# The last 512 MLP features: from two sets of seven products to a plain down projection, half of it woven into the last set and half by token tiles with the final norm and the store

## The reference, cut to what matters

```python
    hf = rms_norm(x, norm_mlp[l])
    x = x + jnp.square(jax.nn.relu(hf @ w_up[l])) @ w_down[l]
return rms_norm(x, norm_final)
```

## Time and profile before

| what | value |
|---|---|
| median of 3 runs | 2890.66 us |
| the profiled execution's own time | 2890.3 us |
| its span (first to last instruction) | 2888.5 us |
| TensorE (PE) busy with matmuls | 98% of the span |
| DVE, ACT, POOL busy | 56%, 35%, 15% |
| mean granted TensorE clock | 0.995 |

### The profile page before, as it was taken

One profiled execution on the slowest core, in us unless ns is written; L12 is line 12 of the kernel. 1 busy time (PEld: TensorE's weight loads), 2 busy tenths in 40 slices (PEclk: granted clock), 3 DMA queues, 4 the chain that ended last, 5 costly groups with the idle time before them and its releaser, 6 DMA issues.

```text
span 2888.5 us, 33862 instructions
## 1 busy us (share of the span) xinstructions
PE 2833.9 (98%) x12753; PEld 2322.8 (80%) x12753; DVE 1626.3 (56%) x2089; ACT 1018.1 (35%) x1383; POOL 431.0 (15%) x262
## 2 busy tenths in 40 slices
PE   8999999999999999999999999999999999999995
PEld 7888877777788888888878888888888888888874
DVE  6212245444325656632344677777677777777677
ACT  6222234333232223322344333333433333343333
POOL 1000000000000000000000332233223331333233
PEclk9999999999999999999999999999999999999998
DMA  7332222322233232553212233223332333223312
GB/s 264 102 102 90 97 90 102 102 87 102 101 117 102 88 109 95 172 177 102 88 59 88 73 117 117 90 96 105 116 104 85 102 116 116 76 98 116 116 59 102
DMA packets 132034, 306.27 MB, mean 106 GB/s; under 512 B 7561, under 2 KB 7674, under 8 KB 129530
## 3 DMA queue, kind: packets, MB, share of 16 engines
q1 hardware_dynamic: 130522, 294.80, 30.6%
q10 hardware_dynamic: 1440, 10.49, 0.9%
HBM read 290.58 MB, written 14.68 MB: 106 GB/s over the span
## 4 chain that ended last, share of the span: by engine, by line
PE 95%; DVE 2%; ACT 1%; issue 1%; DMA 1%; POOL 1%; SPq 0%; POOLq 0%; DVEq 0%; ACTq 0%
PE acc L1603 16%; PE acc L1605 15%; PE acc L1604 15%; PE acc L1931 8%; PE acc L1929 8%; PE acc L1930 8%; PE aux L1949 6%; PE aux L1951 6%; PE aux L1953 6%; PE aux L1624 1%; PE aux L1699 1%; DVE xs L1471 1%; PE aux L1716 1%; PE aux L1698 1%; DMA wide<-in_w_down 0%
## 5 line engine op out<-in xcount | busy, mean ns | idle before, releaser
L981 DVE TENSOR_TENSOR wlo<-raw,whi 128x2048 fp32r<-128x2048 f32 x128 | 293.2, 2290 | 487.3 <-ACT whi L592 486.2
L1603 PE MATMUL acc<-act_hi,whi 128*128 128x512 f32 x1088 | 435.8, 401 | 0.5 <-DVE act_lo L985 0.5
L1605 PE MATMUL acc<-act_hi,wlo 128*128 128x512 f32 x1088 | 424.9, 391 | 0.0
L1604 PE MATMUL acc<-act_lo,whi 128*128 128x512 f32 x1088 | 424.1, 390 | 0.0
L1412 DVE TENSOR_TENSOR flo<-wide,fhi 128x1024 fp32r<-128x1024 f32 x192 | 263.7, 1374 | 250.1 <-ACT fhi L866 250.0
L1929 PE MATMUL acc<-act_hi,fhi 128*128 128x512 f32 x1024 | 398.7, 389 | 0.0
L1931 PE MATMUL acc<-act_hi,flo 128*128 128x512 f32 x1024 | 398.4, 389 | 0.0
L1930 PE MATMUL acc<-act_lo,fhi 128*128 128x512 f32 x1024 | 398.4, 389 | 0.0
L592 ACT ACTIVATE whi<-raw 128x2048 fp32r<-128x2048 f32 x128 | 244.5, 1910 | 436.2 <-PE acc L1605 427.1
L866 ACT ACTIVATE fhi<-wide 128x1024 fp32r<-128x1024 f32 x192 | 203.7, 1061 | 530.4 <-PE acc L1931 363.2
L1949 PE MATMUL aux<-fhi,P_hi 128*128 128x512 f32 x896 | 351.0, 392 | 14.7 <-DVE xs L1471 14.6
(11 more groups left out here) (286 smaller groups left out, 4090.3 us busy)
## 6 DMA issues: line engine op xcount, KB each, us to landing
raw<-in_w_in SPq DMA_DIRECT2D x80, 1024.0 KB, 5.0
raw<-in_w_up SPq DMA_DIRECT2D x64, 1024.0 KB, 5.3
wide<-in_w_down SPq DMA_DIRECT2D x64, 1024.0 KB, 5.2
raw<-in_w_out SPq DMA_DIRECT2D x16, 1024.0 KB, 5.4
gates_scratch<-gate_out ACTq DMA_DIRECT2D x10, 1024.0 KB, 3.9
raw<-in_w_ckv SPq DMA_DIRECT2D x8, 1024.0 KB, 12.1
xs<-in_x SPq DMA_DIRECT2D x8, 1024.0 KB, 13.2
raw<-in_w_attn_br SPq DMA_DIRECT2D x8, 1024.0 KB, 8.2
```

The source lines that it names most:

```text
L981: nc.vector.tensor_tensor(wlo[n % 2][:], raw[n % 4][:], whi[n % 2][:].bitcast(F32), ALU.subtract).then_inc(lo_ready, 1)
L1603: nc.tensor.matmul(dst, s_hi, v_hi, start=first, stop=False)
L1604: nc.tensor.matmul(dst, s_hi, v_lo, start=False, stop=False)
L1605: ins = nc.tensor.matmul(dst, s_lo, v_hi, start=False, stop=last)
```

## The change

Chunk 15 no longer uses the seven products. Its down projection is the plain one: 4 token tiles x 4 feature blocks x 4 column blocks x 3 matmuls.

- **Set 1** of round 7 gets the list `LAST`: its seven products with four units `Y` between and behind them. The `Y` units compute the left half of the outputs (columns 0 to 1023) for chunk 15: 24 matmuls each, into the four `acc` banks, which held the up projection. `Y0` and `Y1` make columns 0 to 511, `Y2` and `Y3` columns 512 to 1023; `land_plain` on DVE adds each of the two halves to `xs` in four pieces.
- **Sets 2 and 3 are gone.** In their place the right half (columns 1024 to 2047) is computed token tile by token tile (`m`): 24 matmuls for each of four tiles, into two banks of its own for each (`z_banks`), from four ring entries z = 0 to 3 that all tiles share. Behind each tile DVE lands it, ACT squares it, POOL makes its inverse root, and the tile is scaled and stored: the left half by ACT (`left_scale`, after DVE multiplied it by the gain), the right by DVE in one operation with the gain (`right_scale`).
- The token operand of the plain product is `hid` split as a whole, `plain_hi` (ACT) and `plain_lo` (DVE), four pieces each. The side sums and splits of chunk 15 and the weight sums of sets 2 and 3 are gone.
- ACT: in set 1 `hidden` stands behind the hi split of P7, at position 4, where it stood ahead of it. DVE: the landings of set 1 are placed by a table `LANDS`, two units behind the product instead of four.
- SP: the four loads of `w_down` for chunk 15 go to slots 0 and 1 during set 0 (in the place of `load_up`), then slot 2 behind P5's split, and slot 3 behind P3's; `gain_f` is loaded between these two. Stores go tile by tile, left then right.

The matmuls from the start of set 1 on are 84 + 96 + 96 = 276 in place of 21 x 12 = 252.

The order, and the banks of the right half:

```diff
+LAST = ("P1", "P2", "P6", "P7", "P5", "Y", "P4", "Y", "P3", "Y", "Y")
+C_LAST = 2 * FF_ROUNDS + 1
...
+    z_banks = (aux[0:2], aux[2:4], acc[0:2], acc[2:4])
```

On SP, in the sets, at the end of the round and behind it:

```diff
+            sp.wait_ge(unit_lo, before + 9)
+            if last and s == 1:
+                load_down(0, C_LAST, 0, 0)
...
+            sp.wait_ge(unit_lo, before + 11)
+            if last and s == 1:
+                load_down(1, C_LAST, 1, 0)
...
+        sp.wait_ge(unit_lo, first + LAST.index("P5") + 1)
+        load_down(2, C_LAST, 0, 1)
+        sp.wait_ge(unit_used, first)
         sp.dma_start(gain_f[:], norm_final.partition_broadcast(P)).then_inc(fin_loaded, 16)
...
+        sp.wait_ge(unit_lo, first + LAST.index("P3") + 1)
+        load_down(3, C_LAST, 1, 1)
+        for t in range(NT):
+            sp.wait_ge(out_left, t + 1)
+            sp.dma_start(out_v[:, t, 0:D // 2], xs[:, t, 0:D // 2]).then_inc(out_stored, 16)
+            sp.wait_ge(out_right, t + 1)
+            sp.dma_start(out_v[:, t, D // 2:D], xs[:, t, D // 2:D]).then_inc(out_stored, 16)
```

On ACT, in the sets and behind them:

```diff
-                if s % 2 and pos == 3 and not (last and s == 3):
+                if s % 2 and pos == (4 if last else 3):
                     hidden(c + 1, first - 1, t)
...
+                if last and s == 1 and name == "P5":
+                    for k in range(4):
+                        act.wait_ge(hid_ready, c * 4 + (4 + k + 1))
+                        nc.scalar.activation(plain_hi[:, k, :], hid[:, k, :], ACT.Copy).then_inc(side_hi, 1)
...
+        for m in range(NT):
+            act.wait_ge(y_landed, NT + m + 1)
+            nc.scalar.activation(junk_l[m][:], xs[:, m, 0:D // 2], ACT.Square, accum_out=x_sums[:, m, 0:1]).then_inc(x3_sq, 1)
...
+        for m in range(NT):
+            for j in range(2):
+                act.wait_ge(z_landed, 2 * m + j + 1)
+                nc.scalar.activation(junk_r[2 * m + j][:], xs[:, m, cols(2 + j, BLK)], ACT.Square,
+                                     accum_out=x_sums[:, m, 1 + j:2 + j]).then_inc(x3_sq, 1)
+            if m:
+                left_scale(m - 1)
+        left_scale(NT - 1)
```

On DVE, the table of landings, and what follows set 1:

```diff
+        LANDS = {"P2": ("P4",), "P6": ("P3",), "P5": ("P1", "P2"), "P4": ("P7",), "P3": (), "Y0": ("P6",), "Y1": ("P5",), "Y2": ("P4",)}
...
+        land_plain(0)
+        for z in range(4):
+            unit_split_lo(set_first(2) + z, wide[2 + z % 2][:, :, cols(z // 2, BLK)], FF_ROUNDS)
+            if z == 0:
+                land("P3", set_first(1) + LAST.index("P3"), 1, FF_ROUNDS)
+        land_plain(1)
...
+        for m in range(NT):
+            dve.wait_ge(z_full, m + 1)
+            for j in range(2):
+                nc.vector.scalar_tensor_tensor(out=xs[:, m, cols(2 + j, BLK)], in0=z_banks[m][j][:], scalar=m_inv[:, m:m + 1],
+                                               in1=xs[:, m, cols(2 + j, BLK)], op0=ALU.mult, op1=ALU.add).then_inc(z_landed, 1)
+            if m == 0:
+                left_gain(0)
+            if m < NT - 1:
+                left_gain(m + 1)
+            dve.wait_ge(x3_sq, NT + 2 * m + 2)
+            nc.vector.reduce_sum(f_sum[:, m:m + 1], x_sums[:, m, 0:3], AX).then_inc(f_stat, 1)
+            if m:
+                right_scale(m - 1)
+        right_scale(NT - 1)
```

On PE, the four token tiles of the right half (its three matmuls for each k are those of the `Y` units):

```diff
+        for m in range(NT):
+            if m < 2:
+                pe.wait_ge(pair_free, landed + 13 + m)
+            else:
+                pe.wait_ge(y_landed, NT + 2 * m - 2)
+            for z in range(4):
+                half, g = z // 2, z % 2
+                n = set_first(2) + z
+                if m == 0:
+                    pe.wait_ge(unit_lo, FF_ROUNDS * PER_ROUND + n + 1)
```

More of the change, by code:

```diff
@@ new lines, in _ @@
+        for s in range(4):
+            down_set(0, s)
+        with sp.Fori(1, FF_ROUNDS) as t:
+            for s in range(4):
+                down_set(t, s)
+        for s in range(2):
+            down_set(FF_ROUNDS, s, last=True)
+        first = FF_ROUNDS * PER_ROUND + set_first(1)
+        sp.wait_ge(unit_lo, first + LAST.index("P5") + 1)
+        load_down(2, C_LAST, 0, 1)
+        sp.wait_ge(unit_used, first)
+        sp.dma_start(gain_f[:], norm_final.partition_broadcast(P)).then_inc(fin_loaded, 16)
@@ L928, in down_set @@
         def down_set(t, s, last=False):
-            first, units, c = set_first(s, last), set_units(s, last), 2 * t + s // 2
+            first, units, c = set_first(s), set_units(s, last), 2 * t + s // 2
             up = 0
@@ L1515, in down_set @@
                         side_split_lo("P3", c)
-                if s % 2 and not last:
+                else:
                     if pos == 5:
@@ new lines, in _ @@
+        up = 0
+        for pos, name in enumerate(LAST):
+            n = set_first(1) + pos
+            for done in LANDS.get(f"Y{up}" if name == "Y" else name, ()):
+                if pos < 3:
+                    land(done, set_first(0) + WITH_UP.index(done), 0, FF_ROUNDS)
+                else:
+                    land(done, set_first(1) + LAST.index(done), 1, FF_ROUNDS)
+            if name == "Y":
+                if up == 0:
+                    for k in range(4):
+                        dve.wait_ge(side_hi, C_LAST * 7 + k + 1)
+                        nc.vector.tensor_tensor(plain_lo[:, k, :], hid[:, k, :], plain_hi[:, k, :].bitcast(F32), ALU.subtract).then_inc(side_lo, 1)
+                unit_split_lo(n, wide[up % 2][:, :, cols(up // 2, BLK)], FF_ROUNDS)
+                up += 1
+            else:
+                unit_split_lo(n, t2[:] if name == "P6" else quarter(1, name), FF_ROUNDS)
@@ L1971, in _ @@
             up_unit(8 + u, u, 1)
-        down_round(0)
+        for s in range(4):
+            down_set(0, s)
         with pe.Fori(1, FF_ROUNDS) as t:
-            down_round(t)
-        down_round(FF_ROUNDS, last=True)
+            for s in range(4):
+                down_set(t, s)
+        for s in range(2):
+            down_set(FF_ROUNDS, s, last=True)
+        landed = 2 + 28 * FF_ROUNDS
+        for m in range(NT):
+            if m < 2:
+                pe.wait_ge(pair_free, landed + 13 + m)
+            else:
+                pe.wait_ge(y_landed, NT + 2 * m - 2)
+            for z in range(4):
+                half, g = z // 2, z % 2
+                n = set_first(2) + z
+                if m == 0:
+                    pe.wait_ge(unit_lo, FF_ROUNDS * PER_ROUND + n + 1)
+                r, bank = n % RING, z_banks[m][half]
+                for i in range(2):
+                    k = 2 * g + i
+                    nc.tensor.matmul(bank[:], plain_hi[:, k, cols(m)], fhi[r][:, i, :], start=k == 0, stop=False)
+                    nc.tensor.matmul(bank[:], plain_hi[:, k, cols(m)], flo[r][:, i, :], start=False, stop=False)
+                    ins = nc.tensor.matmul(bank[:], plain_lo[:, k, cols(m)], fhi[r][:, i, :], start=False, stop=k == 3)
+            ins.then_inc(z_full, 1)
     ctx.close()
```

191 lines of the change are left out of this document (93 added, 98 removed).

## The result

The changed kernel takes **2864.91 us** (median, 2863.91 to 2865.63, 4 runs) against 2890.49 (2890.07 to 2893.11, 4 runs): a ratio of 0.9909, 95% interval 0.9892 to 0.9927. It is 25.6 us faster. The profiled execution has a span of 2863.9 us for the 2888.5 of before.

What follows compares the result with a forecast made beforehand. The prediction took PE as the bound except for 21.1 us lost between products and the tail. Terms +5.4 matmuls, -20.7 lost time and -10.1 tail gave -25.3 us, 2865.4 us, range 2862 to 2876.

Steps and rivals of the forecast that it cites:

- PE's work: Last chunk's matmuls on PE: 168 taken out, 96 + 96 put in, 24 more, +5.4 us.
- The wait at P6: Set 1 of round 7: PE still waits 0.35 us of 1.28, as P7's split on DVE ends behind POOL's T4.
- Y0, the tightest place: First plain unit in set 1: DVE's split ends at 2802.7, PE asks at 2803.0, 0.3 us to spare.
- PE through: Last matmul: PE ends at 2852.05, 15.2 us earlier than 2867.26.
- The tail: Last matmul to the end: 11.2 us for 21.2, since three of four tiles are normed and stored under matmuls.
- POOL's two steps: In the last tile's norm: taken at 2.78 us, with 1.91 as the shorter bound.
- the scaling: DVE's last scaling with the gain, in the tail: taken at 1.22 us, bounds 1.22 and 1.40.
- The sum: Whole kernel: -15.2 and -10.1 make -25.3 us, 2865.4 against the median.
- the 21.1 us: PE time lost between the 21 products of sets 1 to 3: 14.6 us of waits, the rest slower matmuls behind them.
- The first rival: Waits stay in the last set: 1.0 us for each of seven products, +7, 2872; chance 0.08.
- The second rival: The tail stays serial because a step taken as covered isn't: it keeps its 21.2 us, 2875.5; chance 0.06.
- The two slower ones: PE is full, so added work adds time: 2896, chance 0.02; plain matmuls step at 0.43 by the clock: 2904, chance 0.03.

Runs made afterwards that it cites:

- the doubled tile: Changed kernel with the 24 matmuls of token tile 1 done twice, result unchanged: 2869.97 us.
- products in a row: Changed kernel with the last set's seven products in a row, then the four plain units, landings moved to match: 2864.72 us.
- the 11.1 that the run gave: Changed kernel, but DVE waits for all four token tiles before landing the first, so norm and stores follow the last matmul: 2875.06 us.
- moving one line: Kernel before, with DVE's wait for ACT's eight squares moved behind the landing of P7 in the last set: 2884.95 us.
- the first step of the shorter tail: Changed kernel with PE signalling each of a tile's two banks and tile 2's scaling ahead of the last landing: 2863.43 us.
- without side work: Kernel before, without chunk 15's token-side sums and hi/lo splits on ACT and DVE: 2882.93 us.

## Why the prediction was right

**PE's work.** +5.4 us by 24 matmuls of 0.227; the doubled tile showed +5.4.

**The wait at P6.** 0.35 us predicted behind the pace, 0.35 measured (2796.31 for 2795.96), for the reason given: T4 on POOL and then P7's split. Undoing ACT's order gave +0.95 for the 0.9 of the working.

**Y0, the tightest place.** Its split was to end 13.75 us from set 1, wanted at 14.05: measured 13.8 and 14.05. PE did not wait.

**PE through.** 63.1 us from set 1 predicted, 63.0 measured. That term was -15.2 us and came out as -15.3.

**The tail.** 11.2 us predicted, 10.35 measured. The mis-sized term is POOL's two steps: taken at 2.78, the first pair of before, on the ground that DVE has a two-input operation beside it. It has, but for the first step only (1.15 us); the second then ran alone, in 0.55 for 1.60. The sum should have taken the lock once and not the row as a whole; the 1.79 lies even below the lower bound of 1.91. The other terms were off by little: the scaling took 1.28 for 1.22, the last store was issued 0.33 behind it for the 0.25 counted, since SP sends the left half first, and it landed after 3.9 for 3.7.

**The sum.** -25.3 predicted, -25.6 in the medians. By its parts the profiled execution has -15.3 and -10.9, together -26.2, so the forecast was 0.9 short, nearly all of it POOL's steps; its span is only 24.6 shorter because its set 1 began 1.57 later. That the medians meet the forecast within 0.5 us is therefore in part luck: what moves the start of set 1 from one execution to the next, by up to 2.1 us in these profiles, is in no term of the sum.

**What the prediction had wrong is why DVE was late before.** It put the 21.1 us down to a split and a landing for each product plus chunk 15's side work. Its own rows spoke against the first part: 1.21 + 1.40 = 2.61 us is less than 2.72 wherever POOL is idle. The runs show that split and landing do fit by themselves (products in a row), that the side work was a third, and that the wait for the squares and POOL's subtractions were a quarter each. The forecast did not rest on this, since the change takes all three away. The first rival, that waits stay in the last set at 1.0 us for each product, rested on it: it was averaged over all 21 products, while by PE's whole timeline of before about 4.5 of the 21.1 us lay in set 1, and the rest at the starts of sets 2 and 3 and at the wait for the squares, in sets that the change takes out. In set 1 one wait of 0.35 us was left.

The second rival (serial tail) had its price right, 10.1 for the 11.1 that the run gave, and did not come about. The two slower ones did not either: added matmuls are added time now, but the gaps and the tail that went were over five times as much, and no matmul stepped at 0.43 in the plain part.

## What to carry to other kernels

Where a cheaper algorithm (here 7 products for 8) brings side work of other engines with it, compare its last piece, where these engines have the final norm to do as well, with the plain one: 24 more matmuls cost 5.4 us and freed 20.7, of which 5.2 could also be had by moving one line. Put the last output tiles in an order in which each is finished, normed and stored under the next one's matmuls, and then read the last tile's chain step by step: who is queued ahead of it on each engine and in the stores was worth another 2 us of tail. The loss of 21 us on a waiting engine was not one cause here; take such waits apart one by one, since one of them may be a single misplaced line (5.2 us here).

## What the runs showed of the hardware that was not expected

An operation of POOL on one element for each partition takes 0.19 us by itself and 1.15 when DVE runs an operation with two inputs in SBUF beside it (tile 0 and tile 3 in POOL's timeline above; it ends at 2857.34, DVE's scaling at 2857.30). It is 0.19 again for tile 3 in the first step of the shorter tail, where that scaling stands earlier. The Trainium skill (SBUF — State Buffer, "SBUF: two separate sides") has the exclusive lock that would do this; the traces agree with it, in both directions: P7's split waited for T4 as well.

The length of PE's wait alone does not say whether slower matmuls follow. Two waits on the PE timeline with the matmuls behind them, first without side work, then in the kernel before:

```profile
2812.35 0.47 PE L1935 MATMUL aux<-fhi,P_hi 128*128 128x512 f32 x1 [2.43 <-DVE xs L1471]
...
2813.82 0.63 PE L1935 MATMUL aux<-fhi,P_hi 128*128 128x512 f32 x1
```

```profile
2841.77 0.47 PE L1949 MATMUL aux<-fhi,P_hi 128*128 128x512 f32 x1 [2.63 <-DVE xs L1471]
...
2843.00 0.39 PE L1953 MATMUL aux<-fhi,P_lo 128*128 128x512 f32 x1
```

Behind the shorter wait the matmuls last 0.63 us, behind the longer one 0.39. The prediction had the slower matmuls only behind waits of some 3 us. What decides it these runs don't show.

Half the bytes shorten a store's way to landing by far less than half: 2.3 us for the first 256 KB store against 2.6 to 2.7 for a 512 KB one with few in flight, and 3.0 to 3.2 against 3.3 to 4.0 right behind another.
